# The first stack's norms: the next product's first four tiles read un-normalised values times the norm's weight, and the norm is applied to their sums

## The reference, cut to what matters

```python
def layer_norm(x, g, b):
    mu = jnp.mean(xf, -1, keepdims=True)
    var = jnp.mean(jnp.square(xf - mu), -1, keepdims=True)
    return ((xf - mu) * lax.rsqrt(var + LN_EPS)).astype(x.dtype) * g + b
...
for l in range(DEPTH):
    proj = h @ w_in[l]
...
    h = layer_norm(DEEPNORM_ALPHA * h + mixed @ w_out[l], ln1_g[l], ln1_b[l])
    ff = jnp.square(jax.nn.relu(h @ w_up[l])) @ w_down[l]
    h = layer_norm(DEEPNORM_ALPHA * h + ff, ln2_g[l], ln2_b[l])
```

## Time and profile before

| | us |
|---|---|
| median of 3 runs | 1391.33 (1391.18 to 1391.76) |
| profiled execution, its own time | 1391.72 |
| its span, first to last instruction | 1389.7 |
| PE busy in the span | 1362.7 (98%) |
| DVE busy | 1052.0 (76%) |
| ACT busy | 843.5 (61%) |
| POOL busy | 553.1 (40%) |

### The profile page before, as it was taken

How to read it: one execution, slowest core, us unless ns; L and a number is a source line. 1 busy time by engine, 2 the same in 40 slices (tenths; PEclk the granted TensorE clock), 3 DMA queues, 4 the chain that set the end, 5 groups by cost and what they waited for, 6 DMA issues and landing times.

```text
span 1389.7 us, 31502 instructions
## 1 busy us (share of the span) xinstructions
PE 1362.7 (98%) x13386; PEld 1168.5 (84%) x13386; DVE 1052.0 (76%) x1395; ACT 843.5 (61%) x1349; POOL 553.1 (40%) x448
## 2 busy tenths in 40 slices
PE   8999999999999999999999999999999999999997
PEld 7778888888778888888778888888888778988887
DVE  6897886557897884568888898756978865898853
ACT  5684554337675544346896755645788888675652
POOL 0144995122056992224210576603114212366610
PEclk9999999999999999999999999999999999999999
DMA  9543466544343666535335365553643333476551
GB/s 364 185 147 128 170 211 208 198 167 152 123 142 107 239 213 206 189 107 167 122 122 212 143 224 183 176 188 119 213 152 122 100 130 126 150 245 211 194 170 32
DMA packets 37020, 234.65 MB, mean 169 GB/s; under 512 B 4752, under 2 KB 7824, under 8 KB 10384
## 3 DMA queue, kind: packets, MB, share of 16 engines
q1 hardware_dynamic: 36880, 232.63, 48.8%
HBM read 231.57 MB, written 1.05 MB: 167 GB/s over the span
## 4 chain that ended last, share of the span: by engine, by line
PE 76%; DVE 12%; ACT 7%; issue 3%; POOL 1%; DMA 1%; ACTq 0%; DVEq 0%; SPq 0%; POOLq 0%
PE psum L734 22%; PE psum L736 21%; PE psum L735 21%; DVE low L2428 4%; ACT high L1734 2%; PE psum L819 1%; PE psum L820 1%; PE psum L821 1%; ACT m L2136 1%; PE psum L944 1%; DMA raw<-stream 1%; PE psum L940 1%; POOL h L3258 1%; POOL m L3256 1%; DVE arena L2535 1%
## 5 line engine op out<-in xcount | busy, mean ns | idle before, releaser
L2428 DVE SCALAR_TENSOR_TENSOR low<-raw,high 128x2048 f16<-128x2048 f32 (+5 forms) x247 | 533.1, 2165 | 186.1 <-ACT high L1734 185.4
L734 PE MATMUL psum<-u,high 128*128 128x256 f16 (+2 forms) x2008 | 552.7, 275 | 1.3 <-ACT arena L1720 1.3
L736 PE MATMUL psum<-u,low 128*128 128x256 f16 (+2 forms) x2008 | 552.4, 275 | 0.0
L735 PE MATMUL psum<-u,high 128*128 128x256 f16 (+2 forms) x2008 | 552.4, 275 | 0.0
L1734 ACT ACTIVATE high<-raw 128x2048 f16<-128x2048 f32 (+4 forms) x248 | 418.1, 1690 | 122.3 <-PE psum L736 88.6
L734 PE MATMUL psum<-arena,high 128*128 128x256 f16 (+2 forms) x1112 | 304.7, 274 | 1.7 <-DVE arena L2962 1.4
L736 PE MATMUL psum<-arena,low 128*128 128x256 f16 (+2 forms) x1112 | 304.7, 274 | 0.0
L735 PE MATMUL psum<-arena,high 128*128 128x256 f16 (+2 forms) x1112 | 304.7, 274 | 0.0
L734 PEld LDWEIGHTS psum<-u,high 128*128 128x128 f16 x2008 | 196.5, 98 | 34.2 <-issue 5.3
L735 PEld LDWEIGHTS psum<-u,high 128*128 128x128 f16 x2008 | 196.7, 98 | 28.8 <-issue 0.7
L736 PEld LDWEIGHTS psum<-u,low 128*128 128x128 f16 x2008 | 196.6, 98 | 28.1
(11 more groups left out here) (364 smaller groups left out, 1817.7 us busy)
## 6 DMA issues: line engine op xcount, KB each, us to landing
raw<-stream SPq DMA_DIRECT2D x206, 1024.0 KB, 4.8
raw<-stream SPq DMA_DIRECT2D x8, 768.0 KB, 4.2
raw<-stream SPq DMA_DIRECT2D x5, 512.0 KB, 3.6
raw<-stream SPq DMA_DIRECT2D x2, 896.0 KB, 4.5
con<-consts SPq DMA_DIRECT2D x1, 1437.0 KB, 12.3
h<-x_t SPq DMA_DIRECT2D x2, 512.0 KB, 5.8
raw<-stream SPq DMA_DIRECT2D x2, 448.0 KB, 5.2
misc<-small SPq DMA_DIRECT2D x1, 512.0 KB, 14.5
```

What stands on the lines that cost most here:

```text
L734: pe.matmul(out, w_hi, x[0], start=start, stop=False)
L735: pe.matmul(out, w_hi, x[1], start=False, stop=False)
L736: return pe.matmul(out, w_lo, x[0], start=False, stop=stop)
L2428: tell(dve.scalar_tensor_tensor(low[:, at:at + w], raw[:, off:off + w], W_SCALE, high[:, at:at + w], ALU.mult, ALU.subtract), split_ready ...
```

## The change

For m = 0, 1 and 2 the next product's first four output tiles no longer wait for the norm. With y the un-normalised sum, g the norm's weight, mu, r and b its mean, root and bias, W^T((y - mu) r g + b) equals r (W^T(g y) - mu W^T g) + W^T b. So ACT and DVE make the two fp16 parts of g y for each feature tile (`raw_part`, `raw_low`), with two more columns that hold g and b themselves, 258 columns in all. PE runs the first four tiles on them (`abreast_raw`), with the norm's last sums (`finish`) behind feature tile 0, and DVE then mends the four sums in PSUM (`fix_up`). From tile 4 on, products read the normalised operand as before. The 30 matmuls of `keep_awake` at these three places go. `up1` puts tiles 4 and 5 in banks 6 and 7, `in1_1` puts T_GV in bank 6 and T_GV + 1 in bank 1 (before, both products went by banks 0 to 3, T_GV in bank 1 and T_GV + 1 in bank 2). Centring for these norms is now all POOL's. Some semaphores are merged to make room for three new ones; that moves no instruction.

```diff
+UP1_BANKS = [0, 1, 2, 3, 6, 7] + [0, 1, 2, 3] * 6 + [0, 1]
+IN1_RAW_BANKS = [0, 1, 2, 3, 6, 1, 0] + [1, 2, 0] * 3 + [1] + [0] * 4
...
+            def abreast_raw(name, m, sums):
+
+                prod = products[name]
+                for step in prod["steps"][:2]:
+                    await_slot(step[0])
+                    for j in step[1]:
+                        bank_free(prod["first"] + j)
+                for k in range(KT):
+                    pe.wait_ge(raw_ready, raw_value(m, k))
+                    for step in prod["steps"][:2]:
+                        for j in step[1]:
+                            mm = tile(name, step, k, j, lambda k: (rx_hi[:, k, :], rx_lo[:, k, :]), S + 2)
+                            if k == KT - 1:
+                                mm.then_inc(tile_done, 1)
+                    if k == SUMS_BEHIND:
+                        sums()
...
-                    abreast(f"in1_{l}", 2, x_at, operand_ready(3 * l), S, range(KT), AWAKE_1, operand_high(3 * l))
-                one(T_GV)
+                    abreast_raw(f"in1_{l}", 2 * l - 1, ln_sums)
+                one(T_GV, operand_ready(3 * l) if l else None)
                 gate_logits()
-                branch_gates()
+                if l == 0:
+                    branch_gates()
                 one(T_GV + 1)
+                if l:
+                    branch_gates()
...
-                finish()
-                product(f"up1_{l}", x_at, operand_ready(3 * l + 2), S, awake=AWAKE_1, x_high=operand_high(3 * l + 2))
+                abreast_raw(f"up1_{l}", 2 * l, finish)
+                product(f"up1_{l}", x_at, operand_ready(3 * l + 2), S, begun=2, ready_at=4)
...
+            def raw_part(m, which, l, tiles):
...
+                for k in tiles:
+                    tell(act.activation(rx_hi[:, k, 0:S], m_all[:, k, 0:S], ACT.Identity, scale=pcol(f"ln{which}_g{l}", k)), raw_high)
...
                     if t == 3:
                         act.wait_ge(shifted, m + 1)
                         squares(0, 4)
+                        if m < 2 * DEPTH - 1:
+                            raw_part(m, which, l, range(4))
                     if t == 5:
                         squares(4, 6)
+                        if m < 2 * DEPTH - 1:
+                            raw_part(m, which, l, range(4, 6))
...
+                if m < 2 * DEPTH - 1:
+                    raw_part(m, which, l, range(6, KT))
                 act.wait_ge(ln_var, m + 1)
                 inverse_root(bank(4, 0, S), rstd[:, 0:S], eps_ln, rstd[:, 0:S])
+                if m < 2 * DEPTH - 1:
+                    tell(act.activation(rstd[:, 0:S], rstd[:, 0:S], ACT.Exp, scale=-0.5))
...
+                    if l and j < 4:
+                        act.wait_ge(fixed, 4 + j + 1)
...
+                        act.wait_ge(fixed, 8 * l + t + 1)
+                        tell(act.activation(f_relu[:, t, :], bank(BANK[up + t], 0, S), ACT.Relu, scale=-1.0 / W_SCALE, bias=fix_w[:, t, 1:2]),
...
+            def fix_up(name, tiles, biased=()):
...
+                for j in tiles:
+                    dve.wait_ge(tile_done, first + j + 1)
+                    tell(dve.tensor_copy(fix_w[rows[j], j, :], bank(BANK[first + j], S, S + 2, rows[j])))
+                tell.settle()
+                for j in tiles:
+                    acc = bank(BANK[first + j], 0, S, rows[j])
+                    tell(dve.tensor_scalar(fix_w[rows[j], j, 1:2], fix_w[rows[j], j, 1:2], 1.0 / W_SCALE, None, ALU.mult))
+                    tell(dve.scalar_tensor_tensor(acc, root[rows[j], 0:S], fix_w[rows[j], j, 0:1], acc, ALU.mult, ALU.subtract))
+                tell.settle()
+                for j in tiles:
+                    acc = bank(BANK[first + j], 0, S, rows[j])
+                    tell(dve.tensor_tensor(acc, acc, rstd[rows[j], 0:S], ALU.mult), None if j in biased else fixed)
+                    if j in biased:
+                        tell.settle()
+                        tell(dve.tensor_scalar(acc, acc, -1.0 / W_SCALE, fix_w[rows[j], j, 1:2], ALU.mult, ALU.add), fixed)
...
                     tell(dve.scalar_tensor_tensor(m_all[:, t, 0:S], bank(BANK[g], 0, S), 1.0 / W_SCALE, m_all[:, t, 0:S], ALU.mult, ALU.add),
                          *evac_value(g))
+                    if m < 2 * DEPTH - 1:
+                        if t == 5:
+                            raw_low(m, which, l, range(6 if m % 2 else 4))
+                        if t == 6 and m % 2 == 0:
+                            raw_low(m, which, l, range(4, 6))
...
-                low_part(held)
+                if m % 2:
+                    low_part(held)
+                    fix_up(f"in1_{l + 1}", (0, 1))
+                    fix_up(f"in1_{l + 1}", (2, 3), (IN1_NTH[T_GQ + 1],))
+                else:
+                    fix_up(f"up1_{l}", (0, 1))
+                    low_part(held)
+                    fix_up(f"up1_{l}", (2, 3))
...
-                for k in range(KT // 2, KT):
+                for k in range(KT // 2 if m == 2 * DEPTH - 1 else 0, KT):
```

114 lines of the change are left out of this document (78 added, 36 removed).

## The result

The changed kernel takes 1412.43 us, the median of five runs (1410.50 to 1414.02), against 1391.33 us before (1391.18 to 1391.95, five runs). The ratio is 1.0151 with a 95% interval of 1.0136 to 1.0166: 21.1 us slower, where 12.6 were forecast. The profiled execution took 1413.69 us (span 1411.9; before, 1391.72 and 1389.7). In it TensorE's mean granted clock was 0.988 of full speed; before it was 0.999.

The account below looks back on a forecast made before the run. PE, busy 98% of the span, was taken as the bound, so any new wait is paid in full. Two even norms at 2.5 us plus 7.6 for the odd one gave 12.6 us, 1404 us; range 1398 to 1410, 1393 to 1412 with rivals.

Parts of the forecast that it names:

- The sign: Whole kernel: the change was forecast to make it slower, chance 0.78, against 0.04 for the same and 0.18 for faster.
- five gaps of PE that were named: PE waits: raw start about 3 us, tiles 6 and 8 2.5 in all, gate logits 4, T_KC 6 to 7.
- the clock rival: PE's new waits lower its clock at one to three places: 1.5 to 4.5 us more, 1405.5 to 1412; chance 0.20.
- Gap at tile 6: up1, even norms: PE waits 0.5 us for the held slot's low part, out at 151.85 where wanted at 151.35.
- Squares beside POOL's residual: up1, even norms: POOL's 5.38 us operation overlaps DVE's four squares, putting tile 8's low part at 160.1, from 159.1.
- The odd term: m = 1, in1_1: T_KC may start only after T_GV + 1's evacuation at 338.5; +7.6 us, bounds 5 to 9.5.
- the gap ahead of the gate logits: in1_1, m = 1: PE stands 4.1 us behind T_GV until T_LR, mended by fix_up, is out at 325.2.
- the gap at T_KC: in1_1, m = 1: PE waits 6.6 us behind T_GV + 2, as T_KC shares bank 1 with T_GV + 1.
- The even term: m = 0 and 2: DVE's late chain and two fix_ups delay tile 8 of up1; +2.5 us each, bounds 0.8 to 4.5.
- POOL's extra centrings otherwise lie in idle time: POOL at the changed norms: the added centrings were taken to cost nothing further in the sum.
- In between: Rival: even norms win 1 to 2 us each, the odd one loses 3 to 5; 1390 to 1396; chance 0.12.
- the full block: Even norms: exclusive port lock holds DVE's squares until POOL's operation ends at 155.8; even term +2.9 instead of +2.5.

Follow-up runs that it names:

- e1: The changed kernel plus unread matmuls filling PE's four kinds of gaps (raw start, tile 8, gate logits, T_KC): 1410.17 us.
- e4: The kernel before with the change at the odd norm m = 1 only; m = 0 and 2 left as before: 1401.04 us.
- e8: e4 with in1_1's first fix_up (T_LR and T_GK) put ahead of the held slot's low part on DVE: 1399.54 us.
- e7: e4 with banks 1 and 2 swapped from T_KC on, so T_KC no longer waits for T_GV + 1's evacuation: 1396.65 us.
- e5: Change at even norms only, ACT's raw parts put behind the slots, and tile 8's slot (step 4) split sooner: 1398.14 us.
- e6: e5 with POOL's residual scaling cut into eight 128x256 pieces between the low parts of later hidden tiles: 1398.59 us.
- e9: e5 with POOL's two passes behind each even norm made one, (m + b) x ALPHA in place: 1389.38 us.
- e11: e9 with DVE's squares of hidden tiles 0 and 1 ahead of the second fix_up: 1386.38 us.
- e2: The changed kernel with POOL's residual scaling moved from behind the norm to between the 8th and 9th hidden tile of up1: 1415.73 us.
- e12: The change at all three norms, with e11's repairs at the even norms, e7's bank and e8's order at m = 1: 1391.62 us.

## Why the prediction was right and wrong

The sign was right, and the mechanism up to tile 8: the waits moved from the sums to what stands behind the norm on DVE, and of the five gaps of PE that were named all but the one at tile 6 are in the trace. What the even norms cost was not: 2.5 us each were forecast, and even with the clock held up they cost 5.4 and 5.2. 1404 was forecast, 1412.4 came, 2.4 us beyond the forecast's own bounds and 0.4 beyond the end that the clock rival gives. Step by step:

| Step | Predicted | Measured |
|---|---|---|
| Even norms: gap at the raw start | 3.0 us | 2.51 us |
| Copy of the mean, m = 0 | 136.3 | 137.04; 135.78 in e1 |
| fix_up of two tiles | 2.25 us (1.7 to 2.9) | 1.96 us |
| Gap at tile 6 | 0.5 us | none |
| Squares beside POOL's residual | 1.0 us lost (159.1 to 160.1) | 2.6 us lost: 4.89 instead of 2.31 |
| Tile 8 of up1 | 160.1 | 161.43; 160.15 in e1 |
| Each even norm | 2.5 us (0.8 to 4.5) | 7.3 and 6.3; 5.4 and 5.2 in e1 |
| T_LR out, m = 1 (e4) | 325.2, gap 4.1 us | 325.13, gap 3.96 us |
| T_KC (e4) | 338.5, gap 6.6 us | 338.13, gap 3.70 us |
| The odd norm | 7.6 us (5 to 9.5) | 9.1 us; 7.5 in e1, 9.6 by e4 |

**The odd term** was right. Its 7.6 us stand in e1, and 1.5 to 2 us of low clock came on top. One reading of it was half wrong: the gap ahead of the gate logits was put into the account as a loss, but e8 shows that it and the gap at T_KC are one lateness met twice. The sum had used T_KC's start, so it did not count it twice. The gap at T_KC is shorter than forecast (3.47 us, in e4 3.70, for 6.6) though T_KC starts on time: behind the first gap PE worked at 0.50 and came to the second one later. The shared bank was worth 4.4 us (e7), more than the 2.6 us of a tile. A stretch of low clock went with it: behind T_KC's start PE worked 2.87 us at 0.50 in e4, and at 1.00 behind the transposes' start in e7.

**The even term** failed at a step that is a single sentence of the sum: "POOL's extra centrings otherwise lie in idle time". POOL's lateness was priced only for what it does to the squares; behind tile 8 no account was kept, and the wait for POOL's hidden tiles stood at nothing. The chain behind the slot is DVE's square, POOL's two operations for a hidden tile, ACT's relu of tile 6, the bank of tile 10. POOL is free for it at 159.6, where before it was at 148.9, and it is busy or held up in 9.7 of 10 us of up1. Where the clock is kept up, this costs 1.71 us at tile 10 (e1). Where the late slot is repaired, it costs 5.10 us (e5). With the residual out of the way it costs 1.46 (e6, e9), and with the squares of hidden tiles 0 and 1 sooner as well nothing (e11). e2 and e6 show that moving the work is no cure: e6 pays the rest of it in later gaps, of which e9, with the pass taken out, has only 0.60 us left.

**The clock** was the third rival, with 1.5 to 4.5 us on top. It is real: behind six gaps, two at each norm, PE worked at 0.50 to 0.56. It was right as a direction and named the gaps, and its upper end of 1412 is close to the result, and yet it isn't the main part of the miss. Taken away altogether, it gives back 2.3 us of the 21.1 by the medians (with an uncertainty as large), and 4.3 by the two profiles. With the clock kept up e1 is still 18.7 us slower than the kernel before, 6.1 more than the 12.6 of the forecast. At m = 0 the low clock behind tile 8 lost 2.8 us of PE's work, and 1.7 of it only took the place of the wait at tile 10 that e1 has. What it did beyond that was to delay the sums at the start, by 1.3 us, which the whole chain behind them handed on. The Trainium skill (TensorE: Matmul & The Clock Gate, part 1) says that the array falls to 1.2 GHz when it is left idle long enough. The rows above agree: 0.53 behind 2.51 us, 0.50 behind 3.57, 3.96 and 3.47, 1.00 behind 0.72.

**DVE against POOL.** The prediction had POOL's residual run from 150.4 to 155.8, with its end in the squares, and took 160.1 for tile 8. POOL came 3.8 us later: its start 0.8, eight centrings in 6.5 us instead of 5.7, eight bias additions in 9.5 instead of 7.2. Of these last 2.3 us 2.1 are the one addition that the held slot's low part held up (3.03 instead of 0.92). So the residual began just ahead of the squares, and they lost 2.6 us. The Trainium skill (SBUF — State Buffer, section "SBUF: two separate sides") calls the shared port pair an exclusive lock for the whole instruction. By that the squares, which began 0.03 us behind the residual, would have begun to work at 159.6 and ended at 161.9. They ended at 159.16, so here too the wait was shorter than the recorded time of the residual. But it was no sharing either. The first square took 3.89 us where one that POOL doesn't meet takes 0.41 (e2), and the three behind it, still beside the residual as it is recorded, 0.41 each: DVE was held for the first 3.5 us of the 5.37 and then not at all. By the prediction's own times a hold of 3.5 us from 150.4 on ends at 153.9, ahead of its squares at 154.1, so its squares would have lost nothing, and its 1.0 us for the meeting has no ground in these times.

**Three figures** of the prediction do not follow from its own terms. The clock's 1.5 to 4.5 us on 1404 end at 1408.5, not at 1412. In between, even norms that win 1 to 2 each and an odd one that loses 3 to 5 give 1390 to 1394, not 1396. And the full block makes the even term +3.25 with the 2.7 us for the low part that the sum uses, not +2.9. None of them moves the forecast of 1404, but without the first the range would have ended at 1410.

**What stays open.** How much of what the even norms pay is POOL's own time, and how much the holding up between POOL and DVE in up1, isn't parted: e9 takes away both. Whether the odd norm can pay was tried by order and banks only (e12). Other tiles than T_LR and T_GK as the raw ones, so that the gate chain would not wait for a fix_up, would need another packing of the weights and wasn't tried. How the 11.5 us of the even norms divide between clock and POOL differs from run to run by 1 to 2 us, since a gap that is filled by the one is not paid to the other.

## What to carry to other kernels

A gap of the bounding engine that is filled with early work is won only if the engines that prepare the next stage can start that stage as much sooner, with what the early work costs them. So before costing such a change, read the busy share of every helper engine in the stage behind the gap, not in the gap: POOL at 9.69 of 10 us in up1 was the sign that little of what is put on it at the norm would be given back, and it became the bound as soon as the first one was repaired. Read such a share operation by operation, though: an engine that is held up by another one counts as busy, here for some 4 of the 9.69 us by estimate. And count a chain once: where two gaps of the bounding engine hang on one serial chain, closing the first mostly widens the second (e8), while a shared buffer that ties it to that chain is worth most of its wait (3.70 us at T_KC, 1.34 left behind it in e7).

## What the runs showed of the hardware

- Low clock and the next wait cover each other: in the three low stretches shown of the changed kernel alone PE worked 12.2 us (3.61, 5.67 and 2.88) at 0.50 to 0.53, some 6 us of work lost, and holding the clock up in all six (mean 0.999) gave back 2.3 us by the medians, with overlapping intervals. At m = 1 it can be read off: T_KC starts 32.76 us behind down1's end in the changed kernel (345.17 less 312.41) and 32.75 in e1 (343.56 less 310.81), so the low clock behind the first gap cost nothing there.
- POOL's pass in place, (m + b) x ALPHA on 128x256, took 0.47 to 0.76 us for each tile (4.78 for eight, e11), less than the addition alone from m to h, 0.90. Both ran beside DVE's operand chain, so neither is a time alone.
- A square or a low part of DVE that met POOL's 128x2048 scaling was held until 3.5 us behind that one's start and then ran at its own speed, though POOL's operation is recorded as 5.37 us. The time at which it was free is its start plus what it took less what it takes unmet (0.41 us for a square, 2.29 for a low part), an estimate from these rows: changed kernel 154.27 + 3.89 - 0.41 = 157.75, 3.51 behind 154.24; e2 175.39 + 3.64 - 0.41 = 178.62, 3.51 behind 175.11; kernel before 144.15 + 5.15 - 2.29 = 147.01, 3.50 behind 143.51. So the mean of four squares (1.22 us) tells nothing of any of them. What POOL does in the other 1.9 us no row shows.
- The other way round, a POOL operation that met a low part of DVE (2.70 us from 158.31) took 2.60 us from 158.94, where like ones took 0.61 to 0.79: it ended 0.53 us behind the low part's end.
